# Matmuls whose result nobody reads, in seven waits of TensorE

## The reference

```python
def first_block(...):
    h = rms_norm(x, norm_mix_pre[l])
    proj = h @ w_in[l]
    ...
    x = x + rms_norm(merged @ w_o[l], norm_mix_post[l])
    h = rms_norm(x, norm_ffn_pre[l])
    f = (jax.nn.silu(h @ w_ffn_gate[l]) * (h @ w_ffn_up[l])) @ w_ffn_down[l]
    x = x + rms_norm(f, norm_ffn_post[l])

def second_block(...):
    h = modulate(x, sh1, sc1)
    proj = h @ w_in[layer]
    ...
    x = x + g1[:, None, :] * mix
    h = modulate(x, sh2, sc2)
    x = x + g2[:, None, :] * hier_moe(h, w_group, b_group, w_router, b_router, w13, w2)
    return rms_norm_2(x) * final_norm_w
```

## Time and profile before

| | us |
|---|---|
| median of 3 runs | 1300.42 |
| all runs | 1300.42, 1301.64, 1284.38 |
| span of the profiled execution, first to last instruction | 1285.0 |
| median less span | 15.4 |
| TensorE busy, matmul | 1167.4 (91%) |
| VectorE busy | 431.6 (34%) |
| ScalarE busy | 347.3 (27%) |
| POOL busy | 228.9 (18%) |
| mean DMA rate over the span | 246 GB/s |

### The profile page before, as it was taken

The page is one execution under the profiler, slowest core; times in us unless marked ns, Lnnn a source line. Parts: engine busy times, 40 slices in busy tenths (PEclk is TensorE's granted clock), DMA queues, the critical chain, the costliest instruction groups (busy, mean ns, idle before and its releaser), DMA issues.

```text
span 1285.0 us, 16294 instructions
## 1 busy us (share of the span) xinstructions
PE 1167.4 (91%) x6815; PEld 796.8 (62%) x6815; DVE 431.6 (34%) x617; ACT 347.3 (27%) x497; POOL 228.9 (18%) x64
## 2 busy tenths in 40 slices
PE   5899899998997999998899766999999999999995
PEld 4886767777983999986698443444444343333342
DVE  3512733443743645544256631111111111111113
ACT  3331422123603544433635220112111111111111
POOL 1300220000421567764570000000000000000000
PEclk9889999998999999999898986999999999999998
DMA  9433317371336355556241365999999999999990
GB/s 332 136 117 133 130 68 261 132 263 66 132 138 222 119 182 180 182 194 219 101 166 66 134 258 216 361 409 410 410 409 410 410 410 410 410 410 410 409 404 35
DMA packets 119069, 316.67 MB, mean 246 GB/s; under 512 B 7574, under 2 KB 32486, under 8 KB 118886
## 3 DMA queue, kind: packets, MB, share of 16 engines
q1 hardware_dynamic: 114582, 310.90, 64.0%
q10 hardware_dynamic: 4432, 4.97, 1.3%
HBM read 314.80 MB, written 1.05 MB: 246 GB/s over the span
## 4 chain that ended last, share of the span: by engine, by line
PE 68%; SPq 9%; DMA 7%; DVE 7%; ACT 3%; issue 3%; POOL 2%; ACTq 2%; DVEq 0%; POOLq 0%
PE bank L1241 9%; PE bank L687 8%; PE bank L689 8%; PE bank L688 8%; DMA arena<-in_w 7%; SPq L578 7%; PE bank L1267 5%; PE bank L674 5%; PE bank L878 5%; PE bank L1221 4%; PE bank L665 3%; PE bank L1277 3%; SPq L584 2%; PE bank L819 2%; ACTq L1347 1%
## 5 line engine op out<-in xcount | busy, mean ns | idle before, releaser
L1241 PE MATMUL bank<-ring,arena 128*64 128x512 f32 x512 | 226.0, 594 | 15.6 <-DMA arena<-in_w 14.1
L1241 PE MATMUL bank<-arena 128*64 128x512 f32 x512 | 226.0, 594 | 0.0
L518 POOL TENSOR_TENSOR ring_low<-ring,hi_high 128x2048 fp32r<-128x2048 f32 (+3 forms) x27 | 149.5, 5543 | 214.2 <-ACT hi_high L1399 214.2
L689 PE MATMUL bank<-h_high,ring_low 128*128 128x256 f32 x624 | 178.1, 285 | 0.0
L1241 PEld LDWEIGHTS bank<-ring,arena 128*64 128x64 f32 x512 | 68.7, 137 | 165.7 <-issue 134.7
L687 PE MATMUL bank<-h_high,hi_high 128*128 128x256 f32 x528 | 149.3, 283 | 0.0
L688 PE MATMUL bank<-h_low,hi_high 128*128 128x256 f32 x528 | 148.7, 282 | 0.0
L518 DVE TENSOR_TENSOR ring_low<-ring,hi_high 128x2048 fp32r<-128x2048 f32 (+1 forms) x21 | 103.5, 4938 | 98.2 <-ACT hi_high L1399 98.2
L1399 ACT ACTIVATE hi_high<-ring 128x2048 fp32r<-128x2048 f32 (+2 forms) x54 | 96.7, 1847 | 98.0 <-DMA ring<-in_w_ffn_up 45.9
L689 PEld LDWEIGHTS bank<-h_high,ring_low 128*128 128x128 f32 x624 | 121.6, 195 | 0.0
L1267 PE MATMUL bank<-arena 128*64 128x512 f32 x384 | 113.3, 595 | 0.0
(11 more groups left out here) (359 smaller groups left out, 1710.5 us busy)
## 6 DMA issues: line engine op xcount, KB each, us to landing
arena<-in_w SPq DMA_DIRECT2D x112, 1024.0 KB, 18.2
ring<-in_w SPq DMA_DIRECT2D x80, 1024.0 KB, 18.0
ring<-in_w_in SPq DMA_DIRECT2D x15, 2048.0 KB, 7.9
ring<-in_w_ada SPq DMA_DIRECT2D x12, 2048.0 KB, 8.1
ring<-in_w_ffn_gate SPq DMA_DIRECT2D x11, 1024.0 KB, 5.4
ring<-in_w_ffn_up SPq DMA_DIRECT2D x11, 1024.0 KB, 8.0
ring<-in_w_ffn_down SPq DMA_DIRECT2D x5, 2048.0 KB, 7.7
ring<-in_w_o SPq DMA_DIRECT2D x2, 2048.0 KB, 8.0
```

The costliest lines, as they stand in the source:

```text
L518: return eng.tensor_tensor(ring_lo[:, r, c0:c1], ring[:, r, c0:c1], high_of(n)[:, c0:c1].bitcast(F32), ALU.subtract)
L689: return mm(ps, a[1], b[0], start=False, stop=stop)
L1241: last = mm(both(6 + half, x), hg[:, k, x * CAP:(x + 1) * CAP], w13s[x][:, k, half * EF:(half + 1) * EF], start=(k == 0), stop=(k == KD - 1))
```

## The change

A helper keep_busy(ps, n) issues n full matmuls, fp32, identity as weights and the first 512 columns of con as moving operand, into a bank. Nothing reads the results: each is written as the start of a sum, and the real result that follows in the same bank starts its sum anew. It is called at seven places in TensorE's program: in norm_transposes for s = 1, 2 and 3 (7, 10 and 4 matmuls; none for s = 0), ahead of the split products of ("rw", 2) and ("rw", 0) (4 and 5, with a wait for con_in), ahead of the rank counts ("rk",) (5), and ahead of the load of crowded (5), 40 in all. At each, the wait for the bank moves ahead of the added matmuls and the wait for the data stays behind them. No other engine's program changes.

```diff
--- before.py
+++ after.py
@@ -636,9 +636,16 @@
             mm = nc.tensor.matmul
             ident = K("ident")
 
+            def keep_busy(ps, n):
+
+                for _ in range(n):
+                    mm(ps[:, 0:512], ident, con[:, 0:512], start=True, stop=True)
+
             def norm_transposes(s):
                 for kk in range(4):
                     ps = write(pe, ("hT", s, kk))
+                    if kk == 0:
+                        keep_busy(ps, (0, 7, 10, 4)[s])
                     for k2 in range(2):
                         for i in range(NT):
                             if kk == 0 and k2 == 0:
@@ -716,6 +723,9 @@
                     arrived(pe, ("rw", c))
                     feature_major(("rw", j), ("rw", c), 2 * j, 0, 0)
                 else:
+                    if j in (2, 0):
+                        pe.wait_ge(S("con_in"), 16)
+                        keep_busy(write(pe, ("rw", j)), 4 if j == 2 else 5)
                     halved(("rw", c))
                     pe.wait_ge(S("h0_low"), 1)
                     feature_major_by_parts(("rw", j), ("rw", c), 2 * (j % 2), hT_hi[0], hT0_lo)
@@ -1191,8 +1201,9 @@
             last.then_inc(*full(("rt",)))
 
 
+            ps = write(pe, ("rk",))
+            keep_busy(ps, 5)
             pe.wait_ge(S("chosen"), 1)
-            ps = write(pe, ("rk",))
             sel = rtb[4][:, 0:NT * EXPERTS].rearrange("p (i c) -> p i c", i=NT)
             for n, terms in enumerate(((("strict", 0),), (("ones", 0), ("strict", 1)), (("ones", 0), ("ones", 1)))):
                 for j, (name, i) in enumerate(terms):
@@ -1279,6 +1290,7 @@
                     if isinstance(p, int) and p == EP - 1:
                         last.then_inc(S("summed"), 1)
 
+            keep_busy(bank[4], 5)
             pe.wait_ge(S("crowded"), 1)
             many = pe.value_load(crowded[0:1, 0:1])
             with pe.If(many > 0):
```

## The result

The changed kernel takes 1283.15 us (median of 20 runs, 1274.43 to 1292.76) against 1290.62 us of the kernel before (20 runs, 1284.38 to 1303.88). The ratio is 0.9942, 95% interval 0.9914 to 0.9969: 7.5 us less, between 4.0 and 11.1. The runs of both kernels are of two kinds, some 9 to 13 us apart: the lower kind has a median of 1286.34 before and 1279.86 with the change (11 runs each), the upper 1299.37 and 1288.49 (9 runs each).

A forecast was written before the change was run, and what follows sets the result against it. The expert-weight stream at 410 GB/s was taken as the bound, its restart set by TensorE's first expert pair; terms 0 + 0 + 1.2 + 0.8 + 2.2 + 1.0 + 0 = 5.2 us gave 1295.2 us, forecast 1293.5 to 1297, range 1283 to 1304.

The forecast's parts named there:

- gap 7: Wait ahead of the read of crowded: 5 matmuls neither delay load and branch nor gain; 0, upper end 2.5 us.
- The base: Starting time: median 1300.42 us of the runs shown, 15.4 above the profiled span of 1285.0, taken as lying around it.
- Gap 1: Wait ahead of ("rw", 2): the clock holds, but the 2.6 us won become wait for ring_low; worth 0.
- Gap 2: Wait ahead of ("rw", 0): 4.0 us stay idle, so the clock falls; taken at 0, upper end 2.8 us.
- gap 3: Wait in norm_transposes(1): idle rest 1.6 us, the clock holds, transposes run faster; gain 1.2 us, ends 0.4 and 2.6.
- Gap 4: Wait in norm_transposes(2): the clock holds narrowly, ScalarE's eight h_high steps limit; gain 0.8 us, ends 0.4 and 1.6.
- Gap 5: Wait in norm_transposes(3): transposes end 1.7 us earlier, the router's matmuls follow; gain 2.2 us, ends 1.6 and 2.6.
- Gap 6: Wait ahead of ("rk"): L1199 group faster at full clock, with a feared overrun of the fill; gain 1.0 us.
- rival (a): The load of crowded waits for the five matmuls ahead of it: 1299.5 us at full clock, 1303.8 at half; chance 0.2.
- (b): Transposes don't keep the clock up, so the three norm_transposes waits gain nothing: 1299.4 us; chance 0.05.
- (c): The clock also holds in the wait ahead of ("rw", 0): 2.8 us more, 1292.4 us; chance 0.08.
- (d): The fills fail: the clock falls in them or the next wait takes all; 1300.4 us, chance 0.07.

The follow-up runs named there:

- one fill alone: The kernel before with only the five matmuls ahead of the load of crowded, the other calls of keep_busy taken out; ratio 0.9997.
- the attention's fill: Two full matmuls ahead of the attention's second set of scores: on the kernel before 0.996, on the changed kernel 0.9876, with fuller waits too 0.9855.
- the six fills: The changed kernel without the five matmuls ahead of the load of crowded; ratio 0.9938.
- the thin ones: The changed kernel with each of the 40 added matmuls cut from 512 to 8 columns; ratio 0.9972.
- the long fill: The kernel before with a single fill, 12 full matmuls ahead of the load of crowded; one run, 1296.07 us.
- the fuller kernel: The changed kernel plus two matmuls in the attention's wait, with more matmuls in three waits and ScalarE's pooling-weight transfers moved later; median 1278.00 us, ratio 0.9855.

## Why the prediction was right, and where its steps were off

The forecast was a small gain and no more than 2% either way; 5.2 us were forecast and 7.5 measured (4.0 to 11.1). The measured median lies in the range 1283 to 1304 only just, and for a reason of its own, the base. That the two gains are near each other is in part luck. The gaps that were to give the 5.2 us, 3 to 6, gave 3.1; gap 7, forecast at 0, gave 5.6, and some 3 of those have nothing to do with the clock.

**The base.** The step that failed is "15.4 above the span; I take that as what lies around it". It is 1.8 us. The 15.4 set a median of the upper kind against a span of the lower. The execution profiled before was one with the attention at full clock, in the lower kind of run; two of the three times shown were of the upper kind. The 1284.38 "which the profile doesn't explain" was the kind that the profile showed. Sorted by kind, before: 11 of 20 runs at 1284.4 to 1291.1 and 9 at 1296.0 to 1303.9; after: 11 at 1274.4 to 1283.5 and 9 at 1286.9 to 1292.8. The kinds are just as frequent with the change, which doesn't reach the attention. In all nine traces the clock of that stage and the kind of the run's time go together: full in before, one fill alone, and the three with the attention's fill; half in the changed kernel, in the six fills, the thin ones and the long fill.

**What bounds the kernel** was right: the weight stream kept its 410 GB/s, and its restart moved with the first expert matmul, 1.1 us later in both.

**Gap 1** was right: 2.6 us gained and lost again in the wait for ring_low. **Gap 2**: the clock did fall, but 4 us of idle rest were not enough to bring it down before the work went on; it fell into the work, and was back sooner, 1.1 instead of 0. The trace with a rest of 0.6 us shows the whole 2.8. The rule taken from two rows, that what matters is the length of the rest, was too simple: in gap 3 the clock fell behind a rest of only 1.55 us in the changed kernel (0.62 in 427.7 to 431.0), and the gap gave 0.6; in two others with the same fill and the same rest (the six fills and the kernel with the attention's fill) it held and gave the 1.2 predicted. What decides between them isn't shown, and one trace isn't enough to read such a term from.

**Gap 4** was mis-sized: not 0.8 but 0. The step that was wrong is "the eight steps cannot be shorter than 8 x 0.42 = 3.4 and start 0.4 sooner". They start when ScalarE has issued its transfers, 1.6 us after the first transpose (1.5 before), and take 3.75 us (3.76 before), whether the transposes are fast or slow. **Gap 5** measured 1.8 for 2.2. **Gap 6** made L1210 1.05 us shorter as forecast, but VectorE, busy with its two copies until 780.34, became the next to be late, and 0.7 remained. The fill itself held the clock, so the overrun that the prediction feared didn't come. (Its worst end, "a loss of 7", counts 1.0 for that overrun; with its own 3.6 the loss would be 10.)

**Gap 7** was the large error, on the safe side: 0 predicted, 5.6 measured. The disputed part was right: the load passes the queued fills, so rival (a) is out for a fill of five, shown by the sequencer's rows; with twelve the load did begin late. Two things were missed. The hole of 2.3 us was read as part of what a branch costs; it was a place in the code, which eight added instructions moved and the 20 of the fill of gap 7 or the 140 of the other six took away. And "fill 4.3 leaves 2.6 us idle" failed: the clock fell within the fill, which so took 6.22 us and left 0.64, and the clock was back before the gather began. It was the same in all five traces with a fill there: the clock was at half in a part of the fill and at full when the gather began. A fill at full clock throughout would have left the 2.6 us, and no run here shows what the clock does then.

**Rivals.** (b) is out: the transposes ran at 0.12 us behind gaps 4 and 5, 15 in 1.86 us, and the clock was 1.00 in 613.9 to 628.7 and 763.8 to 773.3. (c) came true in part, and wholly in the fuller kernel. (d) is out; the thin matmuls are what it would have looked like.

## What to carry to other kernels

Fill a wait of TensorE only where TensorE itself is late next, leave the shortest rest that the wait's own spread allows, and look at what else stands in the queue of the engine behind it. A wait of 1 us can be worth more than one of 10: here a fill in it kept 15 us of thin matmuls from taking 27. Compare traces by the start of the same instruction when such a stretch sets their spans apart, and runs kind by kind. And before a gain is put down to what was added, put in the same instructions without the work: here they alone gave 3.1 us of the 5.6 at gap 7.

## What the runs showed of the hardware

The attention's matmuls can run through at either clock. In the traces where the clock held they took 15 us at 1.00; in the four where it fell, 0.6 us before their start to 2.1 us behind it, they ran at 0.50 for 27 us or more (27.2 in the changed kernel, busy 27.2 of 27.2 us). The wait of 1.1 us ahead of them is the same in both sorts; what decides isn't shown. Two full matmuls in it (four records, 1.98 us) kept the clock up in the three traces that have them, and of the 22 runs of those kernels none had a time of the upper kind.

The compare-and-branch of TensorE took 6.0 to 6.2 us in the eight traces in which the DMA engines were busy throughout it (share 1.02 to 1.03). With the long fill they went idle halfway through (share 0.49 over it), and it took 4.7 us; that is one trace, and why the branch takes so long isn't shown. The load from SBUF ahead of it took 0.49 us in each. Behind a fill of 10 records the load began 0.1 us after the first; behind one of 24, with the seventh. The Trainium skill, "Advanced Engine Details and Errata", section Control Flow Timing, gives some 108 ns for a compare-and-branch; the changed kernel's trace differs by a factor of 57, and the measurement decides.
